# GpSimd waits while VectorE makes the new x: squares kept in y and added afterwards, the next weights' low parts made by VectorE

## What is computed

```python
def first_block(x, ...):                      # 2 layers
    f = swiglu(rmsnorm(x, ffn1_pre_g[l]), gate, up, down)
    x = x + 0.5 * rmsnorm(f, ffn1_post_g[l])
    m = token_mixing(rmsnorm(x, mix_pre_g[l]), ...)   # band, differential and stick-breaking attention
    x = x + rmsnorm(m, mix_post_g[l])
    f = swiglu(rmsnorm(x, ffn2_pre_g[l]), gate, up, down)
    x = x + 0.5 * rmsnorm(f, ffn2_post_g[l])
def second_block(x, meta_tokens, ...):        # 2 layers
    h = h + rms_norm(mixer(rms_norm(h, pre_g)), post_g)
    h = h + rms_norm(conv_swiglu(rms_norm(h, pre_g)), post_g)
```

## Time and profile before

| | |
|---|---|
| median of 3 runs | 3907.12 us (3905.38 to 3907.83) |
| span of the profiled execution | 3894.2 us |
| mean granted TensorE clock | 0.949 |
| TensorE busy | 3693.2 us (95%), 20446 matmuls |
| VectorE busy | 1855.9 us (48%) |
| ScalarE busy | 1424.5 us (37%) |
| GpSimd busy | 457.8 us (12%) |

### The profile page before, as it was taken

The page is one execution under the profiler, slowest core; times in us unless marked ns, Lnnn a source line. Parts: engine busy times, 40 slices in busy tenths (PEclk is TensorE's granted clock), DMA queues, the critical chain, the costliest instruction groups (busy, mean ns, idle before and its releaser), DMA issues.

```text
span 3894.2 us, 56649 instructions
## 1 busy us (share of the span) xinstructions
PE 3693.2 (95%) x20446; PEld 3061.5 (79%) x20446; DVE 1855.9 (48%) x2698; ACT 1424.5 (37%) x2349; POOL 457.8 (12%) x253
## 2 busy tenths in 40 slices
PE   7999999899999999999899989998999999899998
PEld 6888666678877887665678868768999987689998
DVE  4442467444325432566344334744664347446642
ACT  3222334332323232344333233464343334644432
POOL 2000212100001001211200012112000222120000
PEclk9999899999999999999799998998999989889998
DMA  4332211123323332211123321111222221112222
GB/s 133 94 97 93 71 49 39 55 76 97 95 79 87 95 95 86 68 45 41 44 87 93 96 82 52 41 31 60 89 94 87 77 55 40 35 58 92 88 92 71
DMA packets 329977, 287.81 MB, mean 74 GB/s; under 512 B 9089, under 2 KB 325593, under 8 KB 329781
## 3 DMA queue, kind: packets, MB, share of 16 engines
q1 hardware_dynamic: 327344, 281.63, 24.0%
q10 hardware_dynamic: 2245, 3.50, 0.3%
q0 software_dynamic: 192, 0.14, 0.1%
HBM read 283.10 MB, written 5.27 MB: 74 GB/s over the span
## 4 chain that ended last, share of the span: by engine, by line
PE 88%; DVE 6%; issue 3%; ACT 2%; ACTq 0%; DVEq 0%; POOL 0%; DMA 0%; POOLq 0%
PE ps L460 25%; PE ps L461 24%; PE ps L462 24%; PE ps L948 2%; PE ps L976 2%; DVE x L583 2%; PE ps L965 1%; PE ps L1294 1%; PE ps L492 1%; PE ps L1330 1%; PE ps L502 1%; DVE S L577 1%; ACT xhi L530 1%; PE ps L1291 1%; PE ps L1375 1%
## 5 line engine op out<-in xcount | busy, mean ns | idle before, releaser
L460 PE MATMUL ps<-xhi,whi 128*128 128x264 f32 (+1 forms) x3776 | 1306.5, 346 | 9.0 <-ACT r L522 5.2
L461 PE MATMUL ps<-xlo,whi 128*128 128x264 f32 (+1 forms) x3776 | 1281.2, 339 | 0.0
L462 PE MATMUL ps<-xhi,wlo 128*128 128x264 f32 (+1 forms) x3776 | 1277.7, 338 | 0.0
L443 DVE TENSOR_TENSOR wlo<-raw,whi 128x1024 fp32r<-128x1024 f32 (+1 forms) x426 | 510.8, 1199 | 1340.1 <-ACT whi L437 1337.4
L437 ACT ACTIVATE whi<-raw 128x1024 fp32r<-128x1024 f32 (+1 forms) x536 | 555.4, 1038 | 1367.0 <-PE ps L462 1333.1
L460 PEld LDWEIGHTS ps<-xhi,whi 128*128 128x128 f32 x3776 | 725.8, 192 | 164.8 <-issue 83.6
L462 PEld LDWEIGHTS ps<-xhi,wlo 128*128 128x128 f32 x3776 | 724.9, 192 | 75.7
L461 PEld LDWEIGHTS ps<-xlo,whi 128*128 128x128 f32 x3776 | 726.3, 192 | 73.3 <-issue 1.9
L461 PE MATMUL ps<-hlo,whi 128*128 128x512 f32 (+1 forms) x1408 | 478.4, 340 | 0.0
L460 PE MATMUL ps<-hhi,whi 128*128 128x512 f32 (+1 forms) x1408 | 478.4, 340 | 0.0
L462 PE MATMUL ps<-hhi,wlo 128*128 128x512 f32 (+1 forms) x1408 | 477.3, 339 | 0.0
(11 more groups left out here) (240 smaller groups left out, 3807.7 us busy)
## 6 DMA issues: line engine op xcount, KB each, us to landing
raw<-in_ffn_w_up_dram SPq DMA_DIRECT2D x176, 512.0 KB, 3.6
raw<-in_ffn_w_down_dram SPq DMA_DIRECT2D x120, 512.0 KB, 3.4
raw<-in_w_in_dram SPq DMA_DIRECT2D x94, 512.0 KB, 3.8
raw<-in_ffn_w_gate_dram SPq DMA_DIRECT2D x88, 512.0 KB, 3.8
raw<-in_w_out_dram SPq DMA_DIRECT2D x32, 512.0 KB, 3.5
raw<-in_ffn_w_down_dram SPq DMA_DIRECT2D x24, 256.0 KB, 2.7
tbias_scratch<-rev_scratch ACTq DMA_DIRECT2D x1, 3072.0 KB
y<-tbias_scratch SPq DMA_DIRECT2D x2, 1536.0 KB, 7.2
```

Of the source, the lines that this page charges most:

```text
L443: eng.tensor_tensor(wlo[slot][:, 0:n], raw[slot][:, 0:n], whi[slot][:, 0:n].bitcast(F32), ALU.subtract).then_inc(b.s.weights_split, 1)
L460: pe.matmul(o, wh, hi[:, t0:t0 + w], start=first, stop=False)
L461: pe.matmul(o, wh, lo[:, t0:t0 + w], start=False, stop=False)
L462: ins = pe.matmul(o, wl, hi[:, t0:t0 + w], start=False, stop=last)
```

## The change

ScalarE writes the squares of the new x into y, a chunk each (a chunk of y has been used up when its x is there), and waits for no add. GpSimd's `pool_x` waits for all eight low parts before it adds. In the six handovers inside a layer, the low parts of the next sublayer's first two granules go from GpSimd to VectorE, one before and one after `dve_inv`; ScalarE makes their high parts earlier, the first before the last output pair is taken out and the second between that pair's squares and copies. Since the squares occupy y until they are added, the bias table is loaded by GpSimd's queue after the last add. At the head of the first layer ScalarE waits until the input, which also lies in y, is transposed.

```diff
--- before.py
+++ after.py
@@ -528,12 +528,7 @@
 
             act.wait_ge(b.s.x_new, 8 * sub + c + 1)
             act.activation(xhi[:, c, 0:b.T], xs(b, x, c), ACT.Copy, scale=gain(col, l, c)).then_inc(b.s.x_hi, 1)
-            if c == 0:
-                act.activation(acc[:, 0:b.T], xs(b, x, c), ACT.Square).then_inc(b.s.x_squared, 1)
-            else:
-                if c > 2:
-                    act.wait_ge(b.s.x_summed, 7 * sub + c - 2)
-                act.activation(sq[c % 2][:, 0:b.T], xs(b, x, c), ACT.Square).then_inc(b.s.x_squared, 1)
+            act.activation(y[:, c, 0:b.T], xs(b, x, c), ACT.Square).then_inc(b.s.x_squared, 1)
 
         def dve_operand_lo(dve, b, l, sub, col, c):
             dve.wait_ge(b.s.x_hi, 8 * sub + c + 1)
@@ -542,12 +537,13 @@
                                      op1=ALU.subtract).then_inc(b.s.x_lo, 1)
 
         def pool_x(pool, b, sub):
+            pool.wait_ge(b.s.x_lo, 8 * sub + 8)
             for c in range(1, KD):
                 pool.wait_ge(b.s.x_squared, 8 * sub + c + 1)
                 if c > 1:
                     pool.wait_ge(b.s.x_summed, 7 * sub + c - 1)
-                pool.tensor_tensor(acc[:, 0:b.T], acc[:, 0:b.T], sq[c % 2][:, 0:b.T],
-                                   ALU.add).then_inc(b.s.x_summed, 1)
+                before = y[:, 0, 0:b.T] if c == 1 else acc[:, 0:b.T]
+                pool.tensor_tensor(acc[:, 0:b.T], before, y[:, c, 0:b.T], ALU.add).then_inc(b.s.x_summed, 1)
 
         def pool_y(pool, b, sub):
             for c in range(1, KD - 2):
@@ -557,7 +553,7 @@
                 pool.tensor_tensor(acc[:, 0:b.T], acc[:, 0:b.T], sq[c % 2][:, 0:b.T],
                                    ALU.add).then_inc(b.s.y_summed, 1)
 
-        def act_yevac(act, b, sub, m):
+        def act_yevac(act, b, sub, m, between=None):
 
             for o in range(2):
                 c = 2 * m + o
@@ -566,6 +562,8 @@
                 dst = acc if c == 0 else sq[c % 2]
                 act.activation(tview(b, dst[:, 0:b.T]), pview(b, 4 * (m % 2) + 2 * o),
                                ACT.Square).then_inc(b.s.y_squared, 1)
+            if between is not None:
+                between()
             for o in range(2):
                 ins = act.activation(tview(b, y[:, 2 * m + o, 0:b.T]), pview(b, 4 * (m % 2) + 2 * o), ACT.Copy)
             ins.then_inc(b.s.out_free, 1)
@@ -732,12 +730,12 @@
                 hi_split(i + 1, 0)
                 hi_split(i + 1, 1)
                 hidden(i)
-            act_out(act, b, l, sub, gb + UP_GRAN, f.gb2(l) + UP_GRAN // 2, DOWN_Q, 3)
+            act_out(act, b, l, sub, gb + UP_GRAN, f.gb2(l) + UP_GRAN // 2, DOWN_Q, nxt, 3)
             act_rms(act, b, 2 * sub + 1, SUM_POST)
             if nxt is not None:
                 act_next(act, b, l, sub + 1, *nxt)
 
-        def act_out(act, b, l, sub, gb, gb2, qs, first=2):
+        def act_out(act, b, l, sub, gb, gb2, qs, nxt, first=2):
 
             nq = len(qs)
             n = DOWN_PAIRS * nq
@@ -747,13 +745,19 @@
                 if first <= j + 2 < n:
                     split_hi(act, b, gb + j + 2, gb2 + j // 2 + 1, j % 2, qs[(j + 2) % nq] * PAIR)
                 if j % nq == nq - 1:
+                    between = None
+                    if nxt is not None and j == n - 1:
+                        col, ngb, ngb2 = nxt
+                        split_hi(act, b, ngb(l), ngb2(l), 0)
+                        between = lambda: split_hi(act, b, ngb(l) + 1, ngb2(l), 1)
                     act.wait_ge(b.s.granules_done, gb + j + 1 + CR)
-                    act_yevac(act, b, sub, j // nq)
-
-        def act_next(act, b, l, sub, col, gb, gb2):
-
-            for j in range(2):
-                split_hi(act, b, gb(l) + j, gb2(l), j)
+                    act_yevac(act, b, sub, j // nq, between)
+
+        def act_next(act, b, l, sub, col, gb, gb2, split=False):
+
+            if split:
+                for j in range(2):
+                    split_hi(act, b, gb(l) + j, gb2(l), j)
             for c in range(KD):
                 act_operand(act, b, l, sub, col, c)
 
@@ -845,8 +849,12 @@
             nq = len(qs)
             for j in range(first - 2, DOWN_PAIRS * nq - 2):
                 split_lo(dve, b, gb + j + 2, j % 2, qs[(j + 2) % nq] * PAIR, handover=(qs is OUT_Q and j == 0))
+            if nxt is not None:
+                split_lo(dve, b, nxt[1](l), 0)
             dve_inv(dve, b, 2 * sub + 1)
-            dve_residual(dve, b, l, sub, ch, factor, post, nxt)
+            if nxt is not None:
+                split_lo(dve, b, nxt[1](l) + 1, 1)
+            dve_residual(dve, b, l, sub, ch, factor, post, None if nxt is None else nxt[0])
 
         def pool_first(pool, b, l, gb):
 
@@ -886,12 +894,6 @@
                     g = 3 * p + j
                     src = win1[bass.ds(l * D, D), QKV1[p][j]:QKV1[p][j] + P]
                     load_raw(sp, b, mgb(l) + g, g % 2, src, (8, P))
-                if p == 0:
-
-                    sp.wait_ge(b.s.x_new, 8 * (l * 3 + 1) + 8)
-                    sp.wait_ge(s_tbias, 16)
-                    sp.dma_start(tb,
-                                 tbias_dram[bass.ds(l * 6, 6), :, :].rearrange("h p c -> p h c")).then_inc(s_tb, 16)
             sp_wout(sp, b, l, mgb(l) + 24, wout1)
 
         def sp_wout(sp, b, l, gb, W):
@@ -1091,7 +1093,7 @@
                                              scale=par[:, bass.ds(l + PAR_SUBLN, 1)])
                     ins.then_inc(s.b_hi, 1)
             outputs(7)
-            act_out(act, b, l, sub, mgb(l) + 24, mgb2(l) + 12, OUT_Q)
+            act_out(act, b, l, sub, mgb(l) + 24, mgb2(l) + 12, OUT_Q, nxt)
             act_rms(act, b, 2 * sub + 1, SUM_POST)
             act_next(act, b, l, sub + 1, *nxt)
 
@@ -1216,6 +1218,9 @@
 
         def pool_mix1(pool, l):
 
+            pool.wait_ge(s_tbias, 16)
+            pool.wait_ge(b1.s.x_summed, 7 * (l * 3 + 1) + 7)
+            pool.dma_start(tb, tbias_dram[bass.ds(l * 6, 6), :, :].rearrange("h p c -> p h c")).then_inc(s_tb, 16)
             for g in range(3, 26):
                 split_lo(pool, b1, mgb(l) + g, g % 2, handover=(g == 3))
 
@@ -1577,7 +1582,7 @@
             exps(INVERSE_LATE, 8)
             for i in range(3, 8):
                 hi(i)
-            act_out(act, b, l, sub, g2b(l) + NCOL + 1, g2b2(l) + (NCOL + 1) // 2, OUT_Q)
+            act_out(act, b, l, sub, g2b(l) + NCOL + 1, g2b2(l) + (NCOL + 1) // 2, OUT_Q, nxt)
             act_rms(act, b, 2 * sub + 1, SUM_POST)
             act_next(act, b, l, sub + 1, *nxt)
 
@@ -1952,11 +1957,9 @@
                 pool_first(pool, b1, l, f1.gb)
                 pool_x(pool, b1, l * 3)
                 pool_y(pool, b1, l * 3)
-                pool_first(pool, b1, l, mgb)
                 pool_x(pool, b1, l * 3 + 1)
                 pool_mix1(pool, l)
                 pool_y(pool, b1, l * 3 + 1)
-                pool_first(pool, b1, l, f2.gb)
                 pool_x(pool, b1, l * 3 + 2)
                 pool_y(pool, b1, l * 3 + 2)
 
@@ -1967,7 +1970,6 @@
                 pool_x(pool, b2, l * 2)
                 pool_mix2(pool, l)
                 pool_y(pool, b2, l * 2)
-                pool_first(pool, b2, l, fg.gb)
                 pool_x(pool, b2, l * 2 + 1)
                 pool_y(pool, b2, l * 2 + 1)
 
@@ -1975,12 +1977,13 @@
         def _(act):
             act_setup(act)
             with act.Fori(0, LAYERS) as l:
-                act_next(act, b1, l, l * 3, PAR_FF1PRE, f1.gb, f1.gb2)
+                act.wait_ge(s_xt, KD)
+                act_next(act, b1, l, l * 3, PAR_FF1PRE, f1.gb, f1.gb2, split=True)
                 act_ffn(act, b1, l, f1, nx_m1)
                 act_mix1(act, l, nx_f2)
                 act_ffn(act, b1, l, f2, None)
             with act.Fori(0, LAYERS) as l:
-                act_next(act, b2, l, l * 2, PAR_MIXPRE2, g2b, g2b2)
+                act_next(act, b2, l, l * 2, PAR_MIXPRE2, g2b, g2b2, split=True)
                 act_mix2(act, l, (PAR_FFPRE2, fg.gb, fg.gb2))
                 act_ffn(act, b2, l, fg, None)
 
@@ -1998,8 +2001,8 @@
             with dve.Fori(0, LAYERS) as l:
                 ch.base, n0 = l * CHAIN1, ch.n
                 dve_first(dve, b1, l, l * 3, PAR_FF1PRE)
-                dve_ffn(dve, b1, l, f1, ch, 0.5, PAR_FF1POST, PAR_MIXPRE)
-                dve_mix1(dve, l, ch, PAR_FF2PRE)
+                dve_ffn(dve, b1, l, f1, ch, 0.5, PAR_FF1POST, nx_m1)
+                dve_mix1(dve, l, ch, nx_f2)
                 dve_ffn(dve, b1, l, f2, ch, 0.5, PAR_FF2POST, None)
                 if ch.n - n0 != CHAIN1:
                     raise ValueError(f"CHAIN1 is {ch.n - n0}")
@@ -2008,7 +2011,7 @@
             with dve.Fori(0, LAYERS) as l:
                 ch.base, n0 = l * CHAIN2, ch.n
                 dve_first(dve, b2, l, l * 2, PAR_MIXPRE2)
-                dve_mix2(dve, l, ch, PAR_FFPRE2)
+                dve_mix2(dve, l, ch, (PAR_FFPRE2, fg.gb, fg.gb2))
                 dve_ffn(dve, b2, l, fg, ch, 1.0, PAR_FFPOST2, None)
```

## The result

| | before | changed |
|---|---|---|
| median of the runs | 3907.47 us (4 runs) | 3960.56 us (4 runs, 3947.56 to 3962.45) |
| ratio to before, 95% interval | | 1.0127 [1.0108, 1.0146] |
| span of the profiled execution | 3894.2 us | 3945.9 us |
| granted TensorE clock | 0.949 | 0.946 |
| TensorE, VectorE, GpSimd busy | 3693.2, 1855.9, 457.8 us | 3699.7, 1825.3, 425.3 us |

What follows compares the result with a forecast made beforehand. TensorE was taken to bound the kernel (88% of the chain of waits). Later sum starts of 28 us plus 10 us of clock made 38 us, giving a median of 3945 us (+1.0%), range 3920 to 3974.

Steps and rivals of the forecast that it cites:

- The bound: Whole kernel: 88% of the chain of waits is TensorE, so other engines count only at ten places it waits.
- Part 1: Six handovers inside a layer: residual without GpSimd takes 16.4 us (16.8 for 528 columns), low parts complete 6.5 us earlier.
- Part 2: Seven dependent adds behind the last low part, nothing covered: 9.9 us before the sum, 10.0 for 528 columns.
- The starts of the sum: Ten places where TensorE's square sum begins: shifts from -0.8 to +6.9 us, together 28.0 us slower.
- Part 3: Moved weight splits at six handovers: VectorE's cost nothing, at worst 0.2 us; ScalarE's second delays the norm 0.6 us.
- The clock: TensorE, idle before each sum, loses time at 1.2 GHz: 2.5 us at four places, 10 us together.
- The others lost it already: Places beyond the four charged already lost time to the lower clock, so nothing was charged there.
- Rival 1: Clock reacts no more than it does now: +28 us, 3935 us (3925 with two earlier falls gone); chance 0.16.
- rival 2: Long slow clock stretches at eight places: +73 us in all, with a late table up to 3986 us; chance 0.12.
- Part 4: Bias table on GpSimd's queue after the last add: 0 us charged, bounds 0 and 3 us, twice.
- Rivals 3 and 4: Lone adds much cheaper, 3894 us, chance 0.10; residual's L583 stays long without GpSimd, 3984 us, chance 0.04.

Runs made afterwards that it cites:

- e1: The changed kernel without GpSimd's wait for the eight low parts, so the adds run beside the residual again; 3886.98 us, ratio to before 0.9949.
- e4: The kernel before with only the moved high and low parts of the next weights; 3886.38 us, ratio to before 0.9949.
- e5: The changed kernel with idle matmuls filling the wait before the sum nearly to its end at seven of ten places; 3928.54 us, ratio to before 1.0101.
- e2: The changed kernel with idle matmuls ahead of the sum, 8 in the FFNs, 5 and 4 elsewhere, ending too early; 3940.93 us, ratio to before 1.0105.
- e3: The changed kernel with four GpSimd adds instead of seven, TensorE summing squares 5 to 7 itself; 3919.21 us, ratio to before 1.0048.
- e8: The changed kernel with TensorE summing each chunk's squares at six inner handovers, GpSimd adding elsewhere without the wait; 3921.85 us, ratio to before 1.0070.

## Why the prediction was right, and where its terms were off

**The bound.** Right: TensorE waits at the ten sums, and no other part of the change is seen in the total.

**Part 1, the clean residual.** 16.4 us predicted, 16.38 to 16.40 measured at four handovers of 512 columns; 16.8 predicted and 16.77 measured at two of 528. The step from single clean rows to a period of 1.92 us carried. What it left unsaid e1 and e4 show: in e1 it is 20.8 us from the first scaling (780.65) to the last low part's end (801.42). So of the 6.5 us gained, 2.1 belong to GpSimd's weight splits, and can be had without any wait; 4.4 are what the adds cost VectorE when they run beside it. Laying the adds bare buys 4.4 us for 10.4.

**Part 2, the bare adds.** 9.9 and 10.0 predicted, 10.40 to 10.57 and 10.62 to 10.77 measured from the last low part to the sum. The term was undersized in one place: I charged 0.35 us for the add that meets VectorE's `split_lo`, and it costs 0.8 and more (2.12 us and up, against 1.28 for its neighbours; the terms as listed add up to 9.8, not 9.9). In the view by source line of the changed kernel, L546:

```profile
L546 POOL TENSOR_TENSOR S<-S,y x60: 1261/1295/2162, 37.1 to 3533.6; 128x512 f32<-128x512 f32 x36, 128x528 f32<-128x528 f32 x24
L546 POOL TENSOR_TENSOR S<-y x10: 1282/1298/2324, 35.7 to 3524.5; 128x512 f32<-128x512 f32 x6, 128x528 f32<-128x528 f32 x4
```

The median alone is 1.30 us, as taken; the one that meets the split lasts up to 2.32. The rest is 0.16 us to the first add and 0.05 from the last to the sum. About 0.6 at nine places is 5 us. By the Trainium skill, GPSIMD Engine Reference, section "Elementwise — side-by-side cycle accounting", scaled to 512 columns, an estimate, an add would have been 1.12 us; the shortest of seventy is 1.26, and the measurement decides.

**The starts of the sum.** The sum of shifts was to be 28.0 us; it is 33.4 from root to sum, and 1.4 more for the root itself (0.24 at each of six handovers, where 0.6 was charged for ScalarE's split). Against the list: +3.0 for the second FFN (2.8), +1.6 for the first mixer (0.9), about +4.2 for the second block's FFN (3.6), +3.7 for the first FFN of layer 0 (2.9), +7.8 in layer 1 (6.9), -0.4 and +6.2 for the second block's mixer (-0.8 and +4.4). All in order and each a little short, by the adds. The last was short by 1.8, and its adds explain a third; 0.3 more is a slip, as I let its residual end 1.1 us earlier (3114.10 to 3113.0) where 0.8 stood for the same gain in the first FFN. The same place in the changed kernel:

```profile
3133.39 0.70 DVE L575 SCALAR_TENSOR_TENSOR S<-y,ps 128x528 f32<-128x528 f32 x1 [2.96 <-PE ps L502]
3133.79 5.13 POOL L443 TENSOR_TENSOR wlo<-raw,whi 128x1024 fp32r<-128x1024 f32 x2 [33.86 <-ACT whi L437]
3134.25 2.45 DVE L581 SCALAR_TENSOR_TENSOR x<-S,par,x 128x528 f32<-128x528 f32 x1 [0.15 <-DVE S L575]
```

L575 waited 2.96 us for TensorE's spread (2.29 before), and the first L581 met GpSimd's split from its start (2.45 us), where in the run before it slipped in ahead of it (0.77). When two engines cross there is chance, and I had counted on the order of one execution.

**Part 3, the weights' parts.** Right: VectorE's two splits cost nothing. In layer 0's second FFN L575 follows its root by 1.74 us as before (1.73 in the earlier trace rows). At the first mixers it follows by 2.67 and 2.66 us where it was 2.12 and 2.05, and there too it waits for TensorE's spread and not for a split: in layer 0 the spread itself takes 2.07 us, not 1.56.

**The clock.** Right in kind, and right in size where I charged it: the four places with 2.5 us each cost 3.4, 2.5, 2.5 and 1.9 us more for the sum and the way to r, 10.3 together against my 10. The step that failed is "The others lost it already", which put the other six at nothing. They cost 3.6 us more, 1.6 of it at the second block's mixer of layer 0 and 1.0 at the first FFN of layer 0. Neither had lost the clock before: their sums and ways to r were the fast ones (0.98 and 1.72 us in the FFN, 1.07 and 3.59 in the mixer). The mixer, which I let pass as late by itself, now waits 1.92 us, its matmuls slow down behind the sum, and r comes 5.15 us after its root; e5, whose filling left this wait (1.80), has the same 5.17 us and a granted clock of 0.70 from 2376 to 2380 us, where the kernel before had 1.00 at this point. In the other four, r came late before too (5.9 to 6.7 us after its root), and the part of the step that holds is this: they lose 1.0 us more in all, though their sums take 1.90 to 1.96 us now that took 1.14 to 1.86. I also ended the cost at r. In the first FFN of layer 1 the clock is 0.50 for 6 us behind the sum and 0.72 in the next 6, and from r to the next root it is 2.3 us longer; in layer 0's it is 0.8 us longer.

Rival 1 (no reaction) is refuted by the windows, rival 2 (16 us stretches everywhere) did not come: at the handover shown the clock is back some 9 us after the sum begins. The Trainium skill, TensorE: Matmul & The Clock Gate, section "What's actually happening", has the slow clock as the default, which activity releases; by it I had the term near 20. Against the kernel before, the sums and ways to r take 13.9 us more, between my 10 and those 20; the trace bears out neither in full.

**Part 4, the table.** Right, 0. GpSimd's queue lands it after a median of 7.4 us (7.2 from SP's in the earlier trace rows):

```profile
442.61 0.87 POOL L1223 DMA_DIRECT2D y<-tbias_scratch  x1 [0.70 <-POOL S L546]
...
448.52 0.60 ACT L522 ACTIVATE r<-ps 128x512 f32<-128x512 f32 x1 [4.38 <-PE ps L502]
...
452.74 0.38 DVE L1122 MEMSET y<- 64x384 f32 x1
```

It is there at about 450, and the memset stands at its old distance from r, 4.2 us.

**Rivals 3 and 4.** Neither: an add alone is no cheaper than the trace before had it, and L581 has a median of 0.75 us instead of 0.98.

**The sum.** 38 us forecast, 51.7 between the profiled spans and 53 between the medians. The 13.7 between forecast and spans are 6.8 in the starts, 3.9 in the sums and the ways to r, and 3.0 in the rest of the sublayers. Of that rest the tails of the clock in the two first FFNs would be 3.1, but the first mixers, 5.5 longer and 7.3 shorter, lie in it too, so it cannot be put down to one cause. The largest miss is thus in the starts, mostly the length of the bare adds, and not in the clock. The forecast's median stood 12.9 us above its span, as that of before did; the changed kernel's stands 14.7 above. No kernel tried here was faster than e1 and e4, 0.5% under the kernel before.

## What to carry to other kernels

Two engines that slow each other down are still worth overlapping as long as the slowdown is smaller than the work that is hidden: ask what the overlap costs (here 4.4 us) and what the work costs laid bare (10.4), before making one wait for the other. When a change bundles several edits, price each one; here the moved splits were a gain of 0.5% inside a change that lost 1.3%. And a wait of TensorE can cost more than its length, when what follows runs at 1.2 GHz: here 3.0 to 3.4 us on top of 8.9.

## What the runs showed that I had not expected

- Pauses of TensorE of 2.45 us (e2, e3) already end with the sum at 1.2 GHz, at 1.87 us instead of 1.05; of 0.74 us (e5) and 0.64 us (e1) they do not, at this handover. A short pause is no safety, though: at the second block's FFN of layer 0, e1 waits 0.66 us and its sum takes 1.95 us from start to root, e5 waits 0.84 us and takes 1.14. And in e4, at the handover shown, a wait of 0.63 us leaves the sum fast (1.05 us), but r comes 5.35 us after its root instead of 3.80.
- Busy is not yet fast: in e8 TensorE is busy for 8.00 of 8.00 us (800 to 808) and at 0.50 throughout, with matmuls of one column among those of 512. Whether these are the reason, or something else in that stretch, was not tried.
- VectorE's two-input operation and a GpSimd operation stretch each other in both directions: L581 goes from 0.77 to 2.45 us beside a split, an add from 1.30 to 2.32 beside VectorE's split. The Trainium skill, SBUF — State Buffer, section "Who interferes with whom", has it that a VectorE instruction with two SBUF inputs contends with a GpSimd one that reads SBUF; these rows agree, as does L581's 0.75 with GpSimd at rest.
- The first mixer, 332 to 349 us long over all kernels, differs with the granted clock from one execution of the same kernel to the next (339.3 and 335.0 us in layer 0). What decides it stays open.
